# Joined norms: last tile added on VectorE, outputs scaled beforehand, tiles in pairs, another order between two streams

## The reference, cut to what matters

```python
def rms_norm(x, g):
    xf = x.astype(jnp.float32)
    y = xf * lax.rsqrt(jnp.mean(xf * xf, axis=-1, keepdims=True) + EPS)
    return y.astype(x.dtype) * g

def hybrid_layer(h, hc, ...):
    def pre(t, mm, i, gi):
        return rms_norm(t, g[gi]) * (1 + mm[:, :, i + 1]) + mm[:, :, i]
    def post(t, y, mm, i, gi, wres):
        return t + wres * mm[:, :, i + 2] * rms_norm(y, g[gi])
    h = post(h, swiglu(pre(h, m, 0, 0), ffn_wi[0], ffn_wo[0]), m, 0, 1, 0.5)
    hc = post(hc, swiglu(pre(hc, mc, 0, 0), ffn_wi[0], ffn_wo[0]), mc, 0, 1, 0.5)
    u, uc = pre(h, m, 3, 2), pre(hc, mc, 3, 2)
    ...                       # attention and convolution on u and uc, then the same for 3, 3
    h = post(h, swiglu(pre(h, m, 6, 4), ffn_wi[1], ffn_wo[1]), m, 6, 5, 0.5)
    if not last:
        hc = post(hc, swiglu(pre(hc, mc, 6, 4), ffn_wi[1], ffn_wo[1]), mc, 6, 5, 0.5)
    return h, hc
```

## Time and profile before

| what | value |
|---|---|
| time, median of 3 runs (lowest, highest) | 3189.41 us (3179.52, 3190.13) |
| the profiled execution's own time, its span | 3193.29 us, 3191.5 us |
| mean granted TensorE clock | 0.939 |
| busy: PE, VectorE, ScalarE, GpSimd | 2984.0, 1909.5, 1232.4, 199.2 us |
| share of PE in the chain that ended last | 85% |
| TensorE weight load busy | 2535.4 us |

### The profile page before, as it was taken

How to read it: one execution, slowest core, us unless ns; L and a number is a source line. 1 busy time by engine, 2 the same in 40 slices (tenths; PEclk the granted TensorE clock), 3 DMA queues, 4 the chain that set the end, 5 groups by cost and what they waited for, 6 DMA issues and landing times.

```text
span 3191.5 us, 40778 instructions
## 1 busy us (share of the span) xinstructions
PE 2984.0 (93%) x17016; PEld 2535.4 (79%) x17016; DVE 1909.5 (60%) x2772; ACT 1232.4 (39%) x1579; POOL 199.2 (6%) x206
## 2 busy tenths in 40 slices
PE   6989999999899999999999978899998999997898
PEld 5867887887778878788888658788887888885898
DVE  3246996447479854755753456756657466536554
ACT  3224775344367643322332353222332223335333
POOL 0000000000000000000030113000030000302100
PEclk8778999999789998999989998999989999899899
DMA  7455997456189953343422101444414434231352
GB/s 282 151 198 209 363 358 269 175 209 240 65 334 359 351 188 129 133 164 140 181 95 86 53 14 40 175 148 158 153 66 185 144 153 165 81 112 50 115 194 79
DMA packets 77912, 539.80 MB, mean 169 GB/s; under 512 B 8752, under 2 KB 9008, under 8 KB 18720
## 3 DMA queue, kind: packets, MB, share of 16 engines
q1 hardware_dynamic: 76016, 529.87, 44.6%
q0 software_dynamic: 1712, 7.33, 0.9%
HBM read 536.12 MB, written 1.05 MB: 168 GB/s over the span
## 4 chain that ended last, share of the span: by engine, by line
PE 85%; DVE 6%; ACT 4%; issue 2%; DMA 2%; POOL 1%; SPq 0%; ACTq 0%; DVEq 0%; POOLq 0%
PE bank L999 12%; PE bank L1226 9%; PE bank L1227 9%; PE bank L1228 9%; PE bank L1166 5%; PE bank L1167 5%; PE bank L1168 5%; PE bank L1261 4%; PE bank L1263 4%; PE bank L1262 4%; PE bank L1184 2%; PE bank L1183 2%; PE bank L1185 2%; DMA raw<-in_w_mods 2%; DVE w_lo L1983 1%
## 5 line engine op out<-in xcount | busy, mean ns | idle before, releaser
L1983 DVE TENSOR_TENSOR w_lo<-raw,w_hi 128x2048 fp32r<-128x2048 f32 (+1 forms) x404 | 883.2, 2187 | 279.8 <-ACT w_hi L1546 277.8
L1546 ACT ACTIVATE w_hi<-raw 128x2048 fp32r<-128x2048 f32 (+1 forms) x404 | 738.0, 1828 | 541.9 <-PE bank L1263 256.9
L1226 PE MATMUL bank<-h_hi,w_hi 128*128 128x512 f32 (+1 forms) x1472 | 533.4, 362 | 45.2 <-DVE w_lo L1983 21.1
L1227 PE MATMUL bank<-h_lo,w_hi 128*128 128x512 f32 (+1 forms) x1472 | 528.8, 359 | 0.0
L1228 PE MATMUL bank<-h_hi,w_lo 128*128 128x512 f32 (+1 forms) x1472 | 528.3, 359 | 0.0
L1226 PEld LDWEIGHTS bank<-h_hi,w_hi 128*128 128x128 f32 x1472 | 284.2, 193 | 88.5 <-DVE w_lo L1983 22.4
L1228 PEld LDWEIGHTS bank<-h_hi,w_lo 128*128 128x128 f32 x1472 | 284.3, 193 | 39.8
L1227 PEld LDWEIGHTS bank<-h_lo,w_hi 128*128 128x128 f32 x1472 | 284.8, 193 | 39.0
L2042 DVE CUSTOM_DVE_ANT_0 bank<-raw,raw 128x1024 f32<-128x1024 f32 x240 | 286.3, 1255 | 0.0
L1261 PE MATMUL bank<-act_hi,w_hi 128*128 128x512 f32 (+1 forms) x770 | 271.6, 353 | 1.2 <-DVE w_lo L1983 1.2
L1765 ACT ACTIVATE tmp<-bank 128x512 f32<-128x512 f32 (+1 forms) x88 | 47.8, 543 | 576.4 <-PE bank L1228 576.4
(11 more groups left out here) (454 smaller groups left out, 4691.9 us busy)
## 6 DMA issues: line engine op xcount, KB each, us to landing
raw<-in_w_experts SPq DMA_DIRECT2D x192, 1024.0 KB, 5.6
raw<-in_w_ffn_in SPq DMA_DIRECT2D x88, 1024.0 KB, 4.8
raw<-in_w_mods SPq DMA_DIRECT2D x60, 1024.0 KB, 5.3
raw<-in_w_wide SPq DMA_DIRECT2D x60, 1024.0 KB, 6.9
raw<-in_w_ffn_out SPq DMA_DIRECT2D x64, 704.0 KB, 4.2
raw<-in_w_c_in SPq DMA_DIRECT2D x20, 1024.0 KB, 4.8
raw<-in_w_a_in SPq DMA_DIRECT2D x12, 1024.0 KB, 7.0
raw<-in_w_b_in SPq DMA_DIRECT2D x12, 1024.0 KB, 9.1
```

The source lines that it names most:

```text
L1226: pe.matmul(o, hi[:, f, :], h_hi[:, k, cols], start=(k == 0), stop=False)
L1227: pe.matmul(o, hi[:, f, :], h_lo[:, k, cols], start=False, stop=False)
L1546: act.activation(w_hi[pair_of(k)][:, 0:size], raw_of(k)[:, 0:size], ACT.Copy).then_inc(sem("hi_ready"), 1)
L1983: dve.tensor_tensor(w_lo[pair_of(k)][:, 0:size], raw_of(k)[:, 0:size], w_hi[pair_of(k)][:, 0:size].bitcast(F32), ALU.subtract).then_inc(*r ...
```

## The change

It touches joins alone, on four engines.

1. **Outputs scaled beforehand.** `joint` on ScalarE now makes the square, then a copy of `Y` onto itself with the gain (mark `gained`), then the square of that over all columns. `meet` on VectorE becomes a product of two tiles, waits for `gained`, and stands one chunk later in the program. `scale` needs no gain any more.
2. **Last tile added on VectorE.** For tile 7 VectorE adds all three tiles to the running ones and marks `total`. PE makes the sums once, `all_sums`, in place of `most` and `last`.
3. **Pairs.** `scale`, GpSimd's add, `normed`, ScalarE's upper and `lower` go by pairs of tiles, with one mark for a pair. `BY_TWO` picks single instructions inside a pair for norm, upper and lower; it holds both streams in both of its entries.
4. **Order.** PE's sums and factors of stream 0 come later within stream 1's output, and in `first_two` chunk 0 runs over all 8 tiles of stream 0 before chunk 1. VectorE's and ScalarE's sequences in `join` are written out anew. GpSimd makes all of stream 0's adds before it sums tile 6 of stream 1. The `g_bias` loads wait for the last `h_ready` instead of the last add to `X`.

```diff
+        BY_TWO = ((0, 1), (0, 1))
...
+        by_two = lambda name: BY_TWO[name.startswith("attn")]
...
# GpSimd
                 def add():
-                    k, x = added.pop(0)
-                    cols = tokens((x,))
-                    pool.wait_ge(*W("scaled", (k, x)))
-                    pool.tensor_tensor(X[:, k, cols], X[:, k, cols], Y[:, k, cols], ALU.add).then_inc(*T("x_added", (k, x)))
+                    b, x = added.pop(0)
+                    both, cols = slice(2 * b, 2 * b + 2), tokens((x,))
+                    pool.wait_ge(*W("scaled", (b, x)))
+                    pool.tensor_tensor(X[:, both, cols], X[:, both, cols], Y[:, both, cols], ALU.add).then_inc(*T("x_added", (b, x)))
...
                     if ss == (1,) and j == KT - 2:
-                        add()
-                        add()
+                        for _ in range(KT // 2):
+                            add()
...
# PE
-                def most(self, x):
-                    pe.wait_ge(*W("summed", part_of(self.name, KT - 2, (x,)), at=self.post))
-                    pe.wait_ge(*W("dotted", part_of(self.name, KT - 2, (x,)), at=self.post))
+                def all_sums(self, x):
+                    pe.wait_ge(*W("total", x, at=self.post))
...
-                later = {2: lambda: join.most(1), 3: lambda: join.last(1), 6: lambda: join.factor(1, "y"), 8: lambda: join.factor(1, "x")}
+                later = {5: lambda: join.all_sums(1), 7: lambda: join.factor(1, "y"), 9: lambda: join.factor(1, "x")}
...
-                    lag = 0 if x else LAG
+                    lag = 0 if x else KT if len(ss) == 2 else LAG
...
-                                if (x, c, n, k) == (1, 2, 1, 3):
-                                    join.last(0)
-                                if (x, c, n, k) == (1, 3, 1, 2):
+                                if (x, c, n, k) == (1, 2, 1, 6):
+                                    join.all_sums(0)
+                                if (x, c, n, k) == (1, 3, 0, 2):
+                                    join.factor(0, "y")
+                                if (x, c, n, k) == (1, 3, 0, 6):
                                     join.factor(0, "x")
...
-                                if (j, x, k) == (6, 1, 5):
-                                    join.last(0)
-                                if (j, x, k) == (7, 1, 4):
+                                if (j, x, k) == (6, 1, 9):
+                                    join.all_sums(0)
+                                if (j, x, k) == (7, 1, 2):
+                                    join.factor(0, "y")
+                                if (j, x, k) == (7, 1, 6):
                                     join.factor(0, "x")
...
-                            if (j, x) == (7, 0):
-                                join.most(0)
-                            if (j, x) == (6, 1):
-                                join.factor(0, "y")
...
# ScalarE
-                act.activation(tiles[3 + j % 2 if j else 0][:, cols], Y[:, j, cols], ACT.Square)
+                step(act.activation(tiles[3 + j % 2 if j else 0][:, cols], Y[:, j, cols], ACT.Square))
                 for x in ss:
-                    ins = act.activation(tiles[5 + j % 2 if j else 2][:, tokens((x,))], Y[:, j, tokens((x,))], ACT.Square,
-                                         scale=post2[:, l, i, j, x:x + 1])
-                ins.then_inc(*T("made", (j, ss)))
+                    ins = act.activation(Y[:, j, tokens((x,))], Y[:, j, tokens((x,))], ACT.Copy, scale=post2[:, l, i, j, x:x + 1])
+                ins.then_inc(*T("gained", (j, ss)))
+                act.wait_ge(*W("gained", (j, ss)))
+                act.activation(tiles[5 + j % 2 if j else 2][:, cols], Y[:, j, cols], ACT.Square).then_inc(*T("made", (j, ss)))
...
# VectorE
-                for x in ss:
-                    ins = dve.scalar_tensor_tensor(tiles[1 if j == 0 else 8 if j == KT - 1 else 7][:, tokens((x,))], Y[:, j, tokens((x,))],
-                                                   post2[:, l, i, j, x:x + 1], X[:, j, tokens((x,))], ALU.mult, ALU.mult)
-                if 0 < j < KT - 1:
+                dve.wait_ge(*W("gained", (j, ss)))
+                if j:
+                    dve.wait_ge(*W("dotted", part_of(name, j - 1, ss)))
+                ins = dve.tensor_tensor(tiles[1 if j == 0 else 7][:, cols], Y[:, j, cols], X[:, j, cols], ALU.mult)
+                if j == KT - 1:
+                    dve.wait_ge(*W("summed", part_of(name, KT - 2, ss)))
+                    dve.wait_ge(*W("made", (j, ss)))
+                    dve.tensor_tensor(tiles[0][:, cols], tiles[0][:, cols], tiles[4][:, cols], ALU.add)
+                if j:
                     step(ins)
-                    dve.wait_ge(*W("dotted", part_of(name, j - 1, ss)))
                     ins = dve.tensor_tensor(tiles[1][:, cols], tiles[1][:, cols], tiles[7][:, cols], ALU.add)
                 ins.then_inc(*T("dotted", (j, ss)))
+                if j == KT - 1:
+                    dve.tensor_tensor(tiles[2][:, cols], tiles[2][:, cols], tiles[6][:, cols], ALU.add).then_inc(*T("total", ss[0]))
...
-                def scale(k, x):
-                    cols = tokens((x,))
-                    if k == 0:
+                two_of = lambda bank: bank[:, 0:T1].unsqueeze(1).broadcast_to([P, 2, T1])
+
+                def scale(b, x):
+                    both, cols = slice(2 * b, 2 * b + 2), tokens((x,))
+                    if b == 0:
                         dve.wait_ge(*W("product", ("factor y", x)))
-                    dve.scalar_tensor_tensor(Y[:, k, cols], Y[:, k, cols], post2[:, l, i, k, x:x + 1], chain_bank(x)[0][:, 0:T1],
-                                             ALU.mult, ALU.mult).then_inc(*T("scaled", (k, x)))
+                    dve.tensor_tensor(Y[:, both, cols], Y[:, both, cols], two_of(chain_bank(x)[0]), ALU.mult).then_inc(*T("scaled", (b, x)))
...
+                scale(0, 0)
+                if not two:
+                    scale(1, 0)
+                if two:
+                    if split_from(name) == 4:
+                        dot(5)
+                    split_lo((following, 0))
+                    normed(0, 0)
+                    scale(1, 0)
+                    part(6)
+                    lower(0, 0)
+                    scale(2, 0)
+                    normed(1, 0)
+                    scale(3, 0)
+                    lower(1, 0)
+                    part(7)
+                    normed(2, 0)
+                    dot(6)
+                    normed(3, 0)
+                    lower(2, 0)
+                    dot(7)
+                    lower(3, 0)
+                    split_lo((following, 1))
+                    inverse_y(1)
+                    new_squares(1)
+                    inverse_x(1)
```

More of the change, by code:

```diff
@@ L1643, in post @@
+                    joint(name, 7, (1,))
+                    upper(3, 0)
+                    split_hi((following, 1))
+                    root("y", 1)
+                    root("x", 1)
+                    for b in range(KT // 2):
+                        upper(b, 1)
+                else:
+                    upper(0, 0)
+                    split_hi((following, 1))
+                    for b in range(1, KT // 2):
+                        upper(b, 0)
             def post(name, n):
@@ L2105, in join @@
                 now, stage[0] = stage[0], post
-                two, ni = len(streams(name)) == 2, i_of(norm)
+                two = len(streams(name)) == 2
                 def inverse_y(x):
```

181 lines of the change are left out of this document (89 added, 92 removed).

## The result

The changed kernel takes 3176.25 us (median of 20 runs, 3158.95 to 3182.47), the kernel before 3191.39 us beside it (20 runs, 3179.52 to 3200.08). The ratio of the two sets of runs is 0.9948, with a 95% interval of 0.9934 to 0.9961: about 16.6 us faster (the two medians lie 15.1 us apart). The forecast was 3165 us against 3189.41, a ratio of 0.992. The direction and the range hold; the gain is two thirds of what was forecast.

What follows compares the result with a forecast made beforehand. TensorE, busy 93% of the span, was taken as the bound. Terms -9.1, -15.9 and +0.8 gave -24.2 us: 3193.3 to 3169.1, then 3165 us because the median run lies 3.9 lower; range 3144 to 3186.

Steps and rivals of the forecast that it cites:

- Second parts: Two-stream joins, from the first product needing new `h`, two weight chunks: 35.5 us each, 142.0 against 157.9.
- The bound of 31.2 us: Lower end for each two-stream join after the first `h`: PE bound by its own work, all at full clock.
- First parts: Two-stream joins, old sublayer's end until new `h`: 15.0 us in FFN joins, 21.8 in the second; 9.1 us saved.
- a sign of being wrong: Listed signs against the forecast included PE waiting for VectorE's last add inside stream 1; no size given.
- Nine lots: PE's joint sums in one lot per stream: nine lots fewer, 13.5 to 23 us of PE time.
- Fifth join: Single-stream join: later sums and paired `h` against one lot saved; 0.8 us slower, ends -2 and +3.
- The rest of the span: Outside the joins, last FFN chunks: ScalarE +0.6 us and VectorE -0.3 us a tile, hidden, costed at nothing.
- The rival "given back": Joins: gaps moved, not closed; PE waits longer, clock stays low as long; -9.4 us, 3180 us, chance 0.22.
- The port rival: Joins: GpSimd's pair adds and VectorE's adds and lowers block each other; +21 us, 3210 us, chance 0.12.
- faster: Whole kernel quicker by more than about 0.5% (16 us), the distinguishable difference: chance 0.69; same 0.20, slower 0.11.

Runs made afterwards that it cites:

- the old order alone: Changed kernel with PE's old product order in two-stream joins (chunk 1 three tiles behind chunk 0, early second weight split), one lot and pairs kept: 1.0009.
- the run that empties PSUM first: Changed kernel with VectorE reading a chunk's output tiles out of PSUM before the products and adds, in both attention output projections: 0.9931.
- The norm-first run: Changed kernel with VectorE's scale of both first pairs and norm of the first pair ahead of the first weight split, in two-stream joins: 0.9935.
- The undo: Changed kernel with two lots of sums again, last tile not added on VectorE: 1.0009; repeated with the lots placed earlier: 1.0024.
- light: Changed kernel plus six needless one-column PE products behind tile 3 of stream 0 in each two-stream join: 0.9952.
- heavy: Changed kernel plus five needless 128-column PE products behind tile 3 of stream 0 in each two-stream join: 0.9937.

## Why the prediction was right, and where it was not

- **Second parts, -15.9 forecast, -19.6 measured.** The mechanism held: the old order alone brings the second parts back to 37.7 to 39.0 us. The size, 35.5 us each, was taken as one number where there are two, about 31.2 and 35.7. Three of the four landed on the long one, so that the sum came out near is in part luck. The bound of 31.2 us, reckoned with the clock full, was met with 6.8 us at half clock; in the run that empties PSUM first, second parts of 31.2 us have 3.0 as well as 6.8 us of it. So there PE's own work does not set the length.
- **First parts, -9.1 forecast, -2.8 measured.** This step failed. In the FFN joins I put the pair's add beside the scale and the norms, which "leave room for the adds", and priced it free; it met the weight split that stands between them and took 3.27 us instead of 1.3. The norm-first run took 4.0 us out of the first parts and so shows it. The first lower, too, took 1.24 us beside the next add and not 0.78. In the second join PE's wait for the sums was put at 2 us and was 3.0, and the first `h` came at 25.1 us instead of 21.8, behind the same kind of block (VectorE's split lasted 3.3 us). PE waiting for VectorE's last add was a sign of being wrong, and there it came.
- **Nine lots, 13.5 to 23 us of PE time.** Right in size, wrong in kind. The undo costs 19 to 24 us, and PE's own 1.4 us a lot are only a part of it: late sums in one placing, half clock and a late weight buffer in the other. 1.5 us more of PE's work in each join, light or heavy, made no difference to the time that the runs can tell.
- **Fifth join, +0.8 forecast, +2.9 measured**, inside the bound of +3. The 2 us for later sums were 4.0: VectorE's queue has the products ahead of the tiles' reading, and GpSimd and VectorE stretch each other.
- **The rest of the span, at nothing.** It gave some 8 us back. About 1.2 us behind each two-stream join is the clock; the rest is in untouched code and differs between profiles.
- **The rival "given back"** (3180 us, -9.4) was nearer to the total (-16.6) than its chance of 0.22 suggests: the forecast's -24.2 lies 7.6 us off, the rival 7.2. PE does reach the first `h` earlier and wait longer (3.5 to 3.9 us in the FFN joins where it was 0.8 to 1.7), and three second parts still spend 17 to 18 us at half clock. But its sum is not what happened: it left the second parts almost as they were, and they fell by 19.6 us.
- **The port rival** did not come as a loss: the adds it counted are at 0.42 us, two of stream 0's four pairs of lowers lose 0.77 us a join where it had 1.35 us for each of the four, and where collisions are many (the adds of 512 columns) nothing waits for them. But its mechanism was the one that I had applied too narrowly: an add of 1.30 us took 3.30 beside the split. The Trainium skill, SBUF — State Buffer, section Who interferes with whom, says that a VectorE instruction with two SBUF inputs and a GpSimd instruction that reads SBUF exclude each other. The trace agrees for the weight split, whose two inputs `raw` and `w_hi` lie in SBUF: the add that started 0.16 us behind it ended 1.14 us after it, and the split that started 0.11 us behind an add took 1.03 us more than its 2.29.
- **Chances.** A measured -0.52% stands right at the bound of 0.5% for faster, the case that was given 0.69.

## What to carry to other kernels

When an operation moves, list what runs beside it on the other elementwise engine, not only what it waits for: the long neighbour (here a 2.3 us weight split) sets its price. And where the granted clock has two outcomes for the same code, a stretch has two lengths; forecast both with their shares, and don't credit an edit whose whole gain is a stretch changing from one to the other. A part that gains nothing alone may be needed: undo each part singly before calling it useless.

## What the runs showed of the hardware beyond that

- Needless full products in PE's waits are worth 15 us here (0.9901 against 0.9948), with the clock in the second parts at 0.95 to 1.00 instead of 0.73 to 0.95.
- Two lots of one-column sums 2 us apart were followed by 10 us at half clock with PE busy all the time (8.70 of 8.70 us); one lot, or two lots 3.9 us apart, by 3.4 us in the FFN joins. In the kernel before, lots 3.1 us apart were followed by 10.2 us, and lots 3.5 and 3.6 us apart by 3.4. That a busy engine loses its clock had not been expected. Why six such products later in the join do nothing (light run) stays open.
- The short and long second parts differ by 4.5 us, within one program and from profile to profile. Four such joins can move the total by 18 us, against the 24 us between the fastest and slowest of 20 runs. That they explain this spread was not tested; the two fastest runs (3158.95 and 3159.70 us) had a granted clock of 0.948 and 0.949, the two slowest (3182.47 and 3182.39) 0.938.
